# Five token tiles of 512, 512, 384, 384 and 272 columns, the last third of each FFN tile by tile, and the norms issued in pieces

## What is computed

```
h = x + 0.5 * swiglu(rms_norm(x), ffn1)          # swiglu: (silu(n @ w_gate) * (n @ w_up)) @ w_down
n = rms_norm(h);  z = n @ w_in + b_in            # 7168 columns: u v B C x_in gate_A gate_B
u = gelu(u);  v = layer_norm(gelu(v))
y_a = u * (tril(W_s) v + b)                      # inside chunks of 128 positions, 4 head groups
y_b = B * conv3(C * x_in)                        # causal, carried buffer for the sample group
h = h + (sigmoid(g_a) * y_a + sigmoid(g_b) * y_b) @ w_out
h = h + 0.5 * swiglu(rms_norm(h), ffn2)
y = rms_norm(h, final_norm)                      # after the second layer
```

## Time and profile before

| | us |
|---|---|
| median of 3 runs | 3098.47 (3096.92 to 3100.35) |
| span of the profiled execution, slowest core (5) | 3101.7 |
| TensorE busy | 2939.6 (95%) |
| VectorE busy | 1458.9 (47%) |
| ScalarE busy | 689.3 (22%) |
| GpSimd busy | 450.8 (15%) |

### The profile page before, as it was taken

How to read it: one execution, slowest core, us unless ns; L and a number is a source line. 1 busy time by engine, 2 the same in 40 slices (tenths; PEclk the granted TensorE clock), 3 DMA queues, 4 the chain that set the end, 5 groups by cost and what they waited for, 6 DMA issues and landing times.

```text
span 3101.7 us, 47025 instructions; the slowest of 8 cores (3083.5 to 3101.7 us)
## 1 busy us (share of the span) xinstructions
PE 2939.6 (95%) x16261; PEld 1396.4 (45%) x16261; DVE 1458.9 (47%) x2618; ACT 689.3 (22%) x1090; POOL 450.8 (15%) x566
## 2 busy tenths in 40 slices
PE   5999999899899789999999999989998998999997
PEld 3444444344345344444444444434444444444444
DVE  6232315776677623232363222277667764313236
ACT  3201012322422210101221111133224222010114
POOL 1110100322132101101010101003213221010100
PEclk7999999899999889999999999989999999999998
DMA  9333230597396923214232324238765874242402
GB/s 175 35 35 42 24 52 14 49 97 80 37 88 64 70 34 36 38 20 55 28 41 28 48 28 48 35 35 81 70 76 51 80 63 48 21 55 21 55 1 110
DMA packets 445210, 160.49 MB, mean 52 GB/s; under 512 B 423252, under 2 KB 424532, under 8 KB 444948
## 3 DMA queue, kind: packets, MB, share of 16 engines
q0 software_dynamic: 433280, 136.35, 44.0%
q1 hardware_dynamic: 10480, 20.27, 2.1%
q10 hardware_dynamic: 1220, 0.85, 0.1%
HBM read 285.02 MB, written 8.86 MB: 95 GB/s over the span
## 4 chain that ended last, share of the span: by engine, by line
PE 83%; DVE 9%; issue 2%; DMA 2%; ACT 2%; DVEq 0%; POOL 0%; ACTq 0%; SPq 0%; POOLq 0%
PE pb L217 83%; DVE n L208 3%; DVE sq L200 1%; DVE h L208 1%; DVE vb L200 1%; ACT sq L196 1%; DVE yT L208 1%; DVE vln L205 1%; DMA bvbc<-b_in 1%; DMA xst<-x_prompt 1%; DMA new_conv_sample<-o_107 0%; DMA new_conv_sample<-o_196 0%; ACT vb L701 0%; PE pb L220 0%; DVEq L134 0%
## 5 line engine op out<-in xcount | busy, mean ns | idle before, releaser
L217 PE MATMUL pb<-n,ring 128*128 128x512 bf16 (+1 forms) x10880 | 1957.9, 338 | 5.5 <-DVE yb L208 4.3
L217 PEld LDWEIGHTS pb<-n,ring 128*128 128x128 bf16 x10880 | 908.5, 98 | 1024.8 <-issue 16.2
L200 DVE TENSOR_TENSOR act<-pb,stmp 128x512 bf16<-128x512 f32 (+1 forms) x440 | 250.3, 586 | 978.3 <-PE pb L217 968.4
L217 PE MATMUL pb<-act,ring 128*128 128x512 bf16 (+1 forms) x3520 | 631.5, 337 | 12.9 <-ACT rs L197 6.7
L196 ACT ACTIVATE stmp<-pb 128x512 f32<-128x512 f32 (+1 forms) x440 | 226.3, 515 | 1389.1 <-PE pb L217 1384.8
L217 PEld LDWEIGHTS pb<-act,ring 128*128 128x128 bf16 x3520 | 295.5, 97 | 350.7 <-issue 20.4
L208 DVE SCALAR_TENSOR_TENSOR h<-pb,h 128x512 f32<-128x512 f32 (+1 forms) x560 | 311.2, 585 | 246.9 <-PE pb L217 246.7
L214 POOL DMA_DIRECT2D ring<-w_in x224 | 185.6, 846 | 657.4 <-PE pb L217 656.8
L214 POOL DMA_DIRECT2D ring<-ffn_w_gate x88 | 78.6, 893 | 1079.3 <-PE pb L217 1049.6
L196 ACT ACTIVATE sq<-h 128x2048 f32<-128x2048 f32 (+2 forms) x59 | 108.4, 1838 | 305.4 <-DVE h L208 255.4
L200 DVE TENSOR_TENSOR sq<-sq 128x1024 f32<-128x1024 f32 (+2 forms) x118 | 109.0, 924 | 127.7 <-ACT sq L196 121.5
(11 more groups left out here) (113 smaller groups left out, 1154.5 us busy)
## 6 DMA issues: line engine op xcount, KB each, us to landing
ring<-w_in POOLq DMA_DIRECT2D x224, 256.0 KB, 10.1
ring<-ffn_w_gate POOLq DMA_DIRECT2D x88, 256.0 KB, 5.4
ring<-ffn_w_up POOLq DMA_DIRECT2D x88, 256.0 KB, 7.3
ring<-ffn_w_down POOLq DMA_DIRECT2D x88, 256.0 KB, 4.7
xst<-x_prompt SPq DMA_DIRECT2D x16, 512.0 KB, 10.1
ring<-w_out POOLq DMA_DIRECT2D x32, 256.0 KB, 7.5
y_prompt<-ost SPq DMA_DIRECT2D x16, 512.0 KB, 2.8
bvbc<-b_in SPq DMA_DIRECT2D x4, 512.0 KB, 3.9
```

The source lines that it names most:

```text
L200: return lambda e: e.tensor_tensor(out=out, in0=in0, in1=in1, op=op)
L217: return lambda e: e.matmul(out, lhsT=lhsT, rhs=rhs, start=start, stop=stop)
```

## The change

- `TT` becomes 512, 512, 384, 384, 272: the 16 sample tokens are the end of the last tile, and every per-tile instruction of the sample group is merged into that tile's, but for the convolution's taps, the chunk mixing and v.
- The ring has 18 slots instead of 16, and `GROUPS` is 8, 8, 6. The last group goes tile by tile: for each tile six gate/up blocks, then its down product. The first two blocks of an FFN take tiles 0 and 1 first.
- The norms are split into pieces (squares of two channel blocks, sums, the matmul with Ln and Exp, eight products) which wait in a queue `side`. `work` pops pieces between the matmul groups while an account of TensorE time less VectorE time is positive; `need_n` forces those that the next matmul needs. Layer setup, the sample state's output and its transposes go through the same queue and no stage of their own.
- Buffers lie at fixed places of one arena, and a new one waits only for what lay in its bytes.
- The final norm is made in the last FFN: as soon as a tile is done, 128-token blocks of h are transposed, ScalarE squares them from PSUM with a sum, GpSimd takes the power -0.5, VectorE multiplies from PSUM by it and by the gain, and the row block is stored. From the end of the last third's first tile on, main matmuls have four PSUM banks and the transposes the other four.
- In the mixer the first tap's product goes from VectorE to ScalarE, the chunk mixing's matmuls come after three products rather than one, and the sample tokens' v comes fifth instead of first. The prologue has three load buffers instead of six.

```
-TT = [(0, 512), (512, 512), (1024, 512), (1536, 512), (2048, 16)]
+TT = [(0, 512), (512, 512), (1024, 384), (1408, 384), (1792, 272)]
-NSLOT = 16
-GROUPS = [(0, 6), (6, 14), (14, 22)]
+NSLOT = 18
+GROUPS = [(0, 8), (8, 16), (16, 22)]
+        def work(pe_ns, dve_ns, ahead=3000.0):
+            sst["credit"] = min(sst["credit"] + pe_ns - dve_ns, ahead)
+            sst["since"] += 1
+            while side and sst["credit"] > 0 and sst["since"] >= side[0][1]:
+                sst["credit"] -= pop()
+        def ffn_order(early):
...
+                if gi < len(GROUPS) - 1:
+                    if gi == 0:
+                        ops += [("g", gi, j, t) for j in js[:2] for t in early]
+                        ops += [("g", gi, j, t) for j in js[:2] for t in late]
+                        js = js[2:]
+                    ops += [("g", gi, j, t) for j in js for t in ALL]
+                    ops += [("d", gi, None, t) for t in ALL]
+                else:
+                    for t in ALL:
+                        ops += [("g", gi, j, t) for j in js]
+                        ops.append(("d", gi, None, t))
+            def finish(self, ti):
...
+                push_sq(tt_ns(sz), total)
+                push(0, rstd, lag=2)
+                for c in range(8):
+                    push_out(ti, stt_ns(sz), lambda c=c: out(c), lag=1 if c == 0 else 0)
+        def epi_tile(ti):
+            if not rot["aux"]:
+                rot["main"] = [0, 1, 2, 3]
+                rot["aux"] = [4, 5, 6, 7]
...
+                push(0, trans, lag=2)
+                if len(pend) == 1:
+                    push(1500, pend.pop(0))
+                push(500, stat, lag=2)
+                pend.append(outp)
```

More of the change, by code:

```diff
@@ L267, in build_nc, with sb @@
[L267 to L273, removed]
+        def sb(name, shape, dt):
+            return es.enter_context(nc.sbuf_tensor(name, shape, dt))
+        NT = len(TT)
+        ALL = list(range(NT))
+        h = sb("h", [128, 8, NTOK], F32)
+        hR = [[Res() for _ in TT] for _ in range(8)]
+        n = sb("n", [128, 8, NTOK], BF16)
@@ L300, in mm_group, with push, pop, flush @@
                        reads=reads if i == 0 else (), writes=[bR], signal=(i == nn - 1))
+        side = collections.deque()
+        sst = {"credit": 0.0, "since": 0, "sq": 0}
+        def push(cost, fn, lag=0):
+            side.append((cost, lag, fn))
+        def pop():
+            cost, lag, fn = side.popleft()
+            sst["since"] = 0
+            fn()
+            return cost
+        def work(pe_ns, dve_ns, ahead=3000.0):
[3 more added lines that the diff above has]
+                sst["credit"] -= pop()
+        def flush():
+            while side:
+                pop()
+        def push_sq(cost, fn, lag=0):
+            sst["sq"] += 1
+            def run():
+                sst["sq"] -= 1
+                fn()
+            push(cost, run, lag)
+        npend = [0] * NT
+        def push_out(ti, cost, fn, lag=0):
+            npend[ti] += 1
+            def run():
+                npend[ti] -= 1
+                fn()
+            push(cost, run, lag)
+        def need_n(ti):
+            while npend[ti]:
+                pop()
+        def settle_sq():
+            while sst["sq"]:
+                pop()
+        def tt_ns(sz, ops=1):
+            return ops * (sz / 0.96 + 160)
+        def stt_ns(sz, ops=1):
+            return ops * (sz / 0.96 + 220)
+        def pe_ns(sz, mms=8):
+            return mms * (sz / 2.4 + 2.5)
+        def ffn_order(early):
+            ops = []
+            late = [t for t in ALL if t not in early]
+            for gi, (j0, j1) in enumerate(GROUPS):
+                js = list(range(j0, j1))
+                if gi < len(GROUPS) - 1:
[9 more added lines that the diff above has]
+                        ops.append(("d", gi, None, t))
+            return ops
+        FORD = ffn_order([0, 1])
         specs = []
@@ new lines, in mixer, with tmpbuf @@
+                nv = len(tiles)
+                for ix in range(nv):
+                    stage_a(ix)
+                    if ix >= 1:
+                        stage_b(ix - 1)
+                    if ix >= 2:
+                        stage_c(ix - 2)
+                    work(pe_ns(512, 16), 3250)
+                stage_b(nv - 1)
+                stage_c(nv - 2)
+                stage_c(nv - 1)
+                for (i, _) in wv:
+                    wq.release(i)
+                off = [X0]
+                def tmpbuf(nm, cols):
+                    o = off[0]
+                    off[0] += cols * 4
+                    return ar.buf(nm, o, [128, cols], F32), ar.R(o, cols * 4)
```

1053 lines of the change are left out of this document (506 added, 547 removed).

## The result

| | before | after |
|---|---|---|
| median, same chip, 5 runs each | 3099.42 us | 3017.85 us |
| span of the profiled execution | 3101.7 us | 3013.8 us |
| ratio of after to before, with 95% interval | | 0.9737 (0.972 to 0.9753) |

The changed kernel takes 2.6% less. The forecast was 6.3% less: 2904 us, with a range that ended at 2960. Against the summed span of 2907 the profiled execution is 107 us long; of 195 us forecast on the span, 88 came. Now and then an execution of any of these kernels, before included, runs with one die at a lower clock and some per cent longer: medians take such executions in, ratios leave them out, and for three kernels that had several of them (b3_hold, e3_pop4, c4_best) the times of the other executions are given in place of a median.

A forecast was written before the change was run, and what follows sets the result against it. TensorE, busy 95% of the span, was taken as the bound, with gaps at stage changes. Stream work 2794.5 us plus start 57, gate/up to down 23, clock and small waits 20, end 12.5 gave 2907, less 3.2: 2904 us, range 2872 to 2960.

The forecast's parts named there:

- Prices, tiles, weight loads: Main matmuls: 162.4 ns at 384 columns, 115.6 at 272, weight loads hidden; the new tiles save 50 us.
- The rival with 22 ns more per narrow matmul: Matmuls of 384 or 272 columns don't hide their weight loads, up to 25.6 ns each: 3135 us; chance 0.03.
- Gate/up to down: Last third of the FFNs: TensorE waits about 1.2 us for act before each down product, twenty times: 23 us, bounds 15 and 35.
- Table loads: Ln and Exp among Silu in three FFNs: two 1.28 us loads per tile, taken as 0 because eight banks cover them.
- The next stage starts on tiles 0 and 1, long normed: Stage changes: norms fit beside later tiles' matmuls, so the 153 us of gaps go, less what the new order adds.
- pieces don't move: Norm queue: the account stays low, pieces wait until forced, and 113 us of stage changes return: 3015 us; chance 0.08.
- The start: Prologue up to the first FFN matmul: 57 us instead of 71.9, bounds 50 and 72.
- The clock at the start and small waits: 20 us, 5 of them low clock of the first matmuls, the rest at 4 mixer halves; bounds 5 and 45.
- The sample's v: Mixer: its buffer is used again after the 1.93 us store, twice; 0 to 4 us.
- Weights: Last third holding all 18 slots, with v's rows loaded as slots free up: taken at nothing, a few us a stage if late.
- The end: After the last down product: 12.5 us instead of 43, bounds 10 and 20; transposes in the stream cost 14.6 us.
- The first rival: Norm pieces meet evictions; two table loads for each of five tiles in three FFNs cost 39 us: 2945 us; chance 0.20.

The follow-up runs named there:

- b3_hold: Changed kernel with the norm's Ln and Exp held back during gate/up blocks of a last third, released in down products; 3005.34 and 3006.4 us.
- e3_pop4: Changed kernel with four instead of six norm pieces popped after each chunk in the prologue; 3016.48 to 3036.97 us, ratio 0.9762 to the kernel before.
- c4_best: Changed kernel with lag 0, four early blocks, Ln/Exp hold, four square and six load buffers, sample v last; 2960.73 to 2964.44 us, ratio 0.9553 to before.
- e1_notab: Changed kernel with every norm's Ln and Exp replaced by Identity activations, so no table loads for them; 2980.44 us, ratio 0.9625 to the kernel before.
- c2_lag_early: Changed kernel with lag 0 for squares and sums and an FFN's first four blocks on tiles 0 and 1; 2996.96 us, ratio 0.9664 to before.
- b4_nonorm01: Changed kernel without the norm of tiles 0 and 1 after the mixer's first half; 3009.79 us, ratio 0.9692 to the kernel before.

## Why the prediction was wrong, step by step

- **Prices, tiles, weight loads: right.** 162.5 and 115.8 ns against 162.4 and 115.6; -50 us. The rival with 22 ns more per narrow matmul fell with them. The text had weighed 81 ns at 128 columns from the Trainium skill (TensorE: Matmul & The Clock Gate, Back-to-back issue gap) and stayed with the rows. The same section has a second formula, columns/2.4 + 2.5 ns, by which an estimate is 162.5 and 115.8; it calls it the gap of an isolated matmul, while here streams of thousands run at it.
- **"Gate/up to down", 20 x 1.2 us: right for the bare hand-over** (24.3 over twenty waits in e1_notab, 20.8 in b3_hold). The bound of 35 named what makes it 43 in after, a piece ahead on VectorE; the bound was too low, and what was not named is the lower clock behind most waits of 3.2 and all of 4.3 us.
- **"Table loads. I take 0": the largest miss, 37 us.** The price of the rival, 15 x 2.6 = 39, is near by luck: its fifteen norms cost 29, 2.0 us each, and the other loads, which it didn't count, make up the rest. What failed is the reason to leave it out: the banks that let TensorE run three blocks ahead. They cover a late eviction as long as another product follows. At the end of six blocks nothing follows but the down product that reads `act`, and there the norm's products, late by the loads, stand ahead of it on VectorE. The cover had been taken from the middle of a stage, the delay falls at its edge. The Trainium skill (ScalarE: Activation LUTs, What ACT_TABLE_LOAD costs) gives 1283 ns for a load and 1380 for a drain, 2.66 us a switch. The load agrees (1.28); of the drain the rows show nothing, since Ln begins 1.30 us after its load began.
- **"The next stage starts on tiles 0 and 1, long normed": true, and beside the point.** The wait comes at tile 4. "A tile's norm needs 10 us of VectorE, six blocks give 20.7" set engine time against engine time. The queue counts units, and ten units don't fit into six, whatever they last: 34 us over at three places, of which c2_lag_early gets back 29 there and 17 to 21 on the whole. The text had argued against "pieces don't move" from the credit; the second condition in `work`, `since`, stood in the diff and wasn't weighed.
- **"The start", 57: 23 us too little**, beyond the bound of 72, and 8 later than in the kernel before (71.9), where a gain of 15 had been summed. Copies and norms were added up as VectorE's work, as if always at hand. They are a chain across three engines, through one sum and in TensorE's order, with VectorE idle between its links. "Three load buffers are the risk" named the lesser limit: 2.3 us alone, where the square buffers are 5.5.
- **"The clock at the start and small waits", 20: the mixers' second halves alone take 26**, the first ones nothing. Some 13 are norm pieces in v (b4_nonorm01), which the sum had given no time, and 7 go with the table loads (e1_notab; the two overlap). The rest is open.
- **"The sample's v" and "Weights", taken at nothing: right to a few us.** The waits for vb are 3.7 us in all, and one for the weights of a down product is 1.5.
- **"The end", 12.5: right** (13.3). The transposes in the stream cost less than taken: eight lie between 2922.81 and 2923.68 in after, 0.11 us each against 0.13.
- **Of the marks by which I would be wrong**, one fired (first FFN matmul after 70), and the text's mark of no long idle stretch held. "If ScalarE's rs stands high among the waits" was too narrow a mark: the loads appear as VectorE's `act`, one link on.

The first rival, 2945 us, held the mechanism of the largest term, but the three other misses are not in it. What is shown of them has one error in common: a deferred chain was priced by the busy time of its engines. The trace of before had such a chain in the stage change of the earlier trace rows, with TensorE busy for 36 of 64 us and no engine full.

## What to carry to other kernels

Price work that is put off or cut in pieces by its length in series, from the first piece to the first use of its result, under the rules that release the pieces, and compare that with the cover in the same unit; the busy time of the engines is only a floor. For a detour of an eviction engine, such as a change of its function table, look at the last result before a change of operand: buffers cover a delay in the middle of a stream and not at its edge. And a norm that feeds the next stage is best hidden by the order of the work: tile by tile in the last third was worth 93 us here, more than the tiles.

## What the runs showed of the hardware that I had not expected

A wait of 3.16 us of TensorE was followed by 3.5 us at a granted clock of 0.55, and one of 4.34 us by 48 matmuls that kept 8.43 us where 5.56 is their price; behind the 4.34 us waits of the other two FFNs they kept 8.41 and 8.15. The 3.16 us waits of the first and the third FFN cost another 1.7 and 1.4 us, the 4.34 us ones 2.6 to 2.9. The length alone doesn't decide. The 3.21 us wait of the second FFN was followed by full speed (7.79 us, clock 1.00). The 2.54 us wait of the first FFN was followed by full speed on the profiled core and by 9.2 to 9.4 us instead of 7.80 on cores 0, 2, 4 and 6 of the same execution. And in e1_notab 1.99 us cost nothing in two FFNs and 1.7 us in the third. What decides isn't shown. No wait of 1.8 us or less ahead of a down product was followed by a loss in after or e1_notab.
